# Squares of the RMS norms added on VectorE, and norm factors applied at eviction instead of ahead of the product

## The reference, cut to what matters

```python
def rms_norm(x, g):                       # _rmsnorm is the same
    return x * rsqrt(mean(x * x, -1) + 1e-6) * g

# first block
x = x + 0.5 * gt1 * swiglu(modulate(rms_norm(x, g_ffn1), sh1, sc1), w_gu1, w_down1)   # FFN 1
x = x + gt2 * hybrid_mixer(modulate(rms_norm(x, g_mix), sh2, sc2), ...)
x = x + 0.5 * gt3 * swiglu(modulate(rms_norm(x, g_ffn2), sh3, sc3), w_gu2, w_down2)   # FFN 2
x = rms_norm(x, g_final)
# second block
h = _rmsnorm(x, even_norm);  proj = h @ even_w_in       # 16 column tiles of 128
x = x + even_mixer_rest(proj) @ even_w_out              # pooling, S5 scan, gated product
h = _rmsnorm(x, odd_norm);   proj = h @ odd_w_in        # 24 tiles: value, gate, z
c = conv31(val * sigmoid(gate)) + conv_b                # 31 taps along the sequence
x = x + (silu(layer_norm(c)) * silu(z)) @ odd_w_out
return _rmsnorm(x, final_norm)
```

## Time and profile before

| | |
|---|---|
| median of three runs | 1783.36 us |
| the profiled execution: its time / its span | 1791.0 us / 1789.1 us |
| PE busy | 1632.2 us (91%), 6851 matmuls |
| DVE busy | 865.9 us (48%) |
| ACT busy | 636.8 us (36%) |
| POOL busy | 365.6 us (20%) |
| mean granted clock of PE | 0.95 |

### The profile page before, as it was taken

The page is one execution under the profiler, slowest core; times in us unless marked ns, Lnnn a source line. Parts: engine busy times, 40 slices in busy tenths (PEclk is TensorE's granted clock), DMA queues, the critical chain, the costliest instruction groups (busy, mean ns, idle before and its releaser), DMA issues. The chain is left out here.

```text
span 1789.1 us, 18560 instructions
## 1 busy us (share of the span) xinstructions
PE 1632.2 (91%) x6851; PEld 1203.2 (67%) x6851; DVE 865.9 (48%) x1190; ACT 636.8 (36%) x907; POOL 365.6 (20%) x469
## 2 busy tenths in 40 slices
PE   4899999998999998889999999999899999988377
PEld 2688888886775554235688888888477776766155
DVE  4777246333533335454433433432444344699844
ACT  3322112223335542443433212222442223666442
POOL 3011000000000000002000878510001100799700
PEclk9899999999999997789999999999899999999689
DMA  9677435322321111002233243463032122222101
GB/s 350 192 268 264 144 108 170 94 93 69 93 67 34 36 42 47 1 0 54 61 116 95 97 132 102 128 220 94 24 107 95 49 85 59 84 82 81 37 24 47
DMA packets 202194, 176.33 MB, mean 99 GB/s; under 512 B 6907, under 2 KB 181319, under 8 KB 201606
## 3 DMA queue, kind: packets, MB, share of 16 engines
q1 hardware_dynamic: 186902, 121.87, 22.9%
q0 software_dynamic: 14064, 51.34, 8.2%
q10 hardware_dynamic: 1152, 2.10, 0.3%
HBM read 166.90 MB, written 8.39 MB: 98 GB/s over the span
## 5 line engine op out<-in xcount | busy, mean ns | idle before, releaser
L1706 PE MATMUL ps<-h_hi,w_hi 128*128 128x512 f32 x1224 | 491.8, 402 | 39.4 <-DVE h_lo L1142 27.2
L1707 PE MATMUL ps<-h_lo,w_hi 128*128 128x512 f32 x1224 | 482.6, 394 | 0.0
L1708 PE MATMUL ps<-h_hi,w_lo 128*128 128x512 f32 x1224 | 482.1, 394 | 0.0
L1102 DVE TENSOR_TENSOR w_lo<-w_stage,w_hi 128x1024 fp32r<-128x1024 f32 x225 | 297.5, 1335 | 316.0 <-ACT w_hi L729 313.7
L1706 PEld LDWEIGHTS ps<-h_hi,w_hi 128*128 128x128 f32 x1224 | 233.4, 191 | 112.6 <-issue 64.1
L729 ACT ACTIVATE w_hi<-w_stage 128x1024 fp32r<-128x1024 f32 x225 | 231.0, 1048 | 200.3 <-PE ps L1708 188.3
L1708 PEld LDWEIGHTS ps<-h_hi,w_lo 128*128 128x128 f32 x1224 | 233.2, 191 | 50.2
L1707 PEld LDWEIGHTS ps<-h_lo,w_hi 128*128 128x128 f32 x1224 | 233.6, 191 | 46.6 <-issue 0.2
L1706 PE MATMUL ps<-a_hi,w_hi 128*128 128x512 f32 x544 | 225.4, 414 | 19.2 <-DVE a_lo L1644 12.8
L1707 PE MATMUL ps<-a_lo,w_hi 128*128 128x512 f32 x544 | 214.4, 394 | 0.0
L1708 PE MATMUL ps<-a_hi,w_lo 128*128 128x512 f32 x544 | 214.3, 394 | 0.0
(11 more groups left out here) (365 smaller groups left out, 1612.1 us busy)
## 6 DMA issues: line engine op xcount, KB each, us to landing
w_stage<-in_w_gu SPq DMA_DIRECT2D x88, 512.0 KB, 4.4
ada_w<-in_w_ada POOLq DMA_DIRECT2D x72, 512.0 KB, 6.4
w_stage<-in_w_down SPq DMA_DIRECT2D x44, 512.0 KB, 3.7
w_stage<-in_w_in SPq DMA_DIRECT2D x24, 512.0 KB, 3.8
w_stage<-in_odd_w_in SPq DMA_DIRECT2D x24, 512.0 KB, 3.7
w_stage<-in_even_w_in SPq DMA_DIRECT2D x16, 512.0 KB, 3.9
w_stage<-in_w_out SPq DMA_DIRECT2D x8, 512.0 KB, 4.0
mats<-mats_d POOLq DMA_DIRECT2D x4, 1024.0 KB, 7.8
```

What stands on the lines that cost most here:

```text
L1102: dve.tensor_tensor(w_lo[:, c % RING], w_in[:, c % RING], w_hi[:, c % RING].bitcast(F32), ALU.subtract).then_inc(w_split, 1)
L1706: pe.matmul(bank, w_hi[:, slot, k], rhs_hi, start=start, stop=False, skip_group_check=True)
L1707: pe.matmul(bank, w_hi[:, slot, k], rhs_lo, start=False, stop=False, skip_group_check=True)
L1708: return pe.matmul(bank, w_lo[:, slot, k], rhs_hi, start=False, stop=stop, skip_group_check=True)
```

## The change

- `square` now writes the first square into `rs` and the later ones into `sq`; DVE adds them there (`add_square`) for norms 1, 2, final, odd and last, and PE does two matmuls with ones per norm (`norm_total`) instead of eight. The table of functions is loaded ahead of the first square.
- End of FFN 2: ACT writes `h_hi` from the unnormalised `xT` times `gg` (final gain times even gain) and two squares per tile, for the final and for the even norm; DVE adds both kinds and writes `h_lo` (`scaled_lo`). The even mixer starts with these rows. Both factors come from one chain of Ln and Exp (`final_and_even_rs`), DVE writes the normalised `xT` and the common factor, and DVE takes all 16 tiles from PSUM with a multiplication by it (`take`). ACT's Silu then works in place.
- Odd mixer: its first two tiles (gate, value) are made from unnormalised rows in the same way and multiplied by the factor when taken; normalised rows are written into the upper half of `cv` and into `h_hi`, `h_lo` for the other 22 tiles.
- Last norm: ACT multiplies `xT` by the gain, PE transposes the tiles within the output product (`turn_out`), the sums are taken by rows (eight small matmuls with one column), and the factor per row is applied as the banks are copied out. The four stores take 256 columns of all 512 rows each instead of 128 full rows.

The diff, cut to its core (indentation reduced):

```diff
@@ -478,10 +497,11 @@
     load(0, T_ODD + n, cols_of(a["odd_w_in_2"][0], [D, 0, 2 * D][n % 3] + n // 3 * P))
 for n in range(KT):
     load(0, T_OOUT + n, rows_of(a["odd_w_out_2"][0], n))
-for st in range(ST):
-    sp.wait_ge(out_copied[0], st + 1)
-    sp.wait_ge(out_copied[1], st + 1)
-    sp.dma_start(out[st * P:(st + 1) * P, :], o_rows[:, st]).then_inc(out_stored, 16)
+for c in range(ST):
+    sp.wait_ge(out_copied[0], c + 1 if c < ST - 1 else ST + 1)
+    sp.wait_ge(out_copied[1], min(c + 1, ST - 1))
+    at = slice(c * 2 * P, (c + 1) * 2 * P)
+    sp.dma_start(out.rearrange("(t p) d -> p t d", p=P)[:, :, at], o_rows[:, :, at]).then_inc(out_stored, 16)
 sp.wait_ge(out_stored, 16 * ST)
...
+def two_squares(kt):
+    if kt == 0:
+        act.preload_act_table_set("natural_log_exp_and_others")
+    if kt >= 2:
+        act.wait_ge(sq_added, added(N_EVEN, kt - 1))
+    act.activation(rs[:] if kt == 0 else sq[:, 0], xT[:, kt], ACT.Square).then_inc(sq_ready, 1)
+    act.activation(tmp[:, 0] if kt == 0 else sq[:, 1], xT[:, kt], ACT.Square,
+                   scale=cols[:, G_FINAL + kt:G_FINAL + kt + 1]).then_inc(sq_ready, 1)
...
+def scaled_hi(kt, g):
+    act.activation(h_hi[:, kt], xT[:, kt], ACT.Copy, scale=g[:, kt:kt + 1]).then_inc(h_hi_ready, 1)
...
-    act.wait_ge(sq_used, (n + 1) * KT)
-    act.activation(rs[:], ps[0][:], ACT.Ln, bias=eps[:], scale=1.0 / D).then_inc(ln_ready, 1)
...
+        act.preload_act_table_set("natural_log_exp_and_others")
+        act.wait_ge(sq_used, KT)
+    else:
+        act.wait_ge(sq_used, SUMMED[n])
+    act.activation(rs[:], ps[3 if n == N_ODD else 0][:], ACT.Ln, bias=eps[:], scale=1.0 / D).then_inc(ln_ready, 1)
...
+def final_and_even_rs():
+    act.wait_ge(sq_used, SUMMED[N_FIN])
+    act.activation(tmp2[:, 0], ps[0][:], ACT.Ln, bias=eps[:], scale=1.0 / D).then_inc(ln_ready, 1)
+    act.wait_ge(ln_ready, N_FIN + 1)
+    act.activation(tmp2[:, 1], tmp2[:, 0], ACT.Exp, scale=-1.0).then_inc(fin_chain, 1)
+    act.wait_ge(fin_chain, 1)
+    act.activation(tmp2[:, 0], tmp2[:, 0], ACT.Exp, scale=-0.5).then_inc(rs_ready, 1)
+    act.wait_ge(fin_chain, 2)
+    act.activation(tmp2[:, 1], tmp2[:, 1], ACT.Ln, bias=eps[:], scale=1.0 / D).then_inc(ln_ready, 1)
+    act.wait_ge(ln_ready, N_EVEN + 1)
+    act.activation(tmp2[:, 1], tmp2[:, 1], ACT.Exp, scale=-0.5).then_inc(rs_ready, 1)
...
@@ -781,7 +838,13 @@
                     act.wait_ge(wb_stored[par], 16 * 4)
             for kt in range(KT):
                 act.wait_ge(x_new, X_FFN[n] + KT + kt + 1)
-                square(norm_after, kt)
+                if norm_after == N_FIN:
+                    if kt == 0:
+                        act.wait_ge(gs_ready, 4)
+                    scaled_hi(kt, gg)
+                    two_squares(kt)
+                else:
+                    square(norm_after, kt)
         hi(0, t1 + 12)
...
-            act.activation(us[:, n], bank, ACT.Copy).then_inc(even_read, 1)
         elif n < 12 and n % 2 == 0:
-            act.activation(zp[(n - 4) // 2], bank, ACT.Silu).then_inc(even_read, 1)
-        elif n < 12:
-            g = (n - 5) // 2
-            act.wait_ge(pads_zero, 1)
-            upto(act, pool_mixed, g - 1)
-            act.activation(pv[:, g % 2, 16:], bank, ACT.Copy).then_inc(even_read, 1)
-        else:
-            act.activation(zs[:, n - 12], bank, ACT.Silu).then_inc(even_read, 1)
+            act.wait_ge(even_read, n + 1)
+            act.activation(zp[(n - 4) // 2], zp[(n - 4) // 2], ACT.Silu).then_inc(z_ready, 1)
+        elif n >= 12:
+            act.wait_ge(even_read, n + 1)
+            act.activation(zs[:, n - 12], zs[:, n - 12], ACT.Silu).then_inc(z_ready, 1)
         t = n - 2
         if 0 <= t < 4:
...
-    for n in range(3 * KT):
+    for n in range(2):
         hi(0, T_ODD + n + 2)
+    norm_rs(N_ODD)
+    for kt in range(KT):
+        act.wait_ge(hn_ready, 3 * KT + kt + 1)
+        if kt < KT - 1:
+            act.wait_ge(pair_read, kt + 1)
+        else:
+            act.wait_ge(w_used, T_ODD + 2)
+        act.activation(h_hi[:, kt], cv[:, 4 + kt % 4], ACT.Copy).then_inc(h_hi_ready, 1)
+    act.wait_ge(odd_read, 1)
+    act.activation(tmp[:, 0], tmp[:, 0], ACT.Tanh, scale=0.5).then_inc(odd_read, 1)
...
@@ -1062,24 +1131,25 @@
 norm_rs(2)
 modulate(2, sublayer(2)[1])
 ffn(1, N_FIN, set_up)
-norm_rs(N_FIN)
...
+final_and_even_rs()
 even_mixer()
 project_out(T_EOUT, X_EVEN, N_ODD)
-norm_rs(N_ODD)
-modulate(4, None)
 odd_mixer()
 for kt in range(KT):
     act.wait_ge(x_new, X_ODD + kt + 1)
     square(N_LAST, kt)
-norm_rs(N_LAST)
-for st in range(ST):
-    act.wait_ge(out_t, KT)
-    act.activation(o_rows[:, st, 0:S], ps[2 * st][:], ACT.Copy).then_inc(out_copied[0], 1)
+    act.activation(xT[:, kt], xT[:, kt], ACT.Copy, scale=cols[:, G_LAST + kt:G_LAST + kt + 1]).then_inc(fin_ready, 1)
+act.wait_ge(sq_used, SUMMED[N_LAST])
+act.activation(rcol[:], ps[7][:, 0:ST], ACT.Ln, bias=eps[:], scale=1.0 / D).then_inc(ln_ready, 1)
+act.wait_ge(ln_ready, N_LAST + 1)
+act.activation(rcol[:], rcol[:], ACT.Exp, scale=-0.5).then_inc(rs_ready, 1)
+act.wait_ge(rs_ready, N_LAST + 1)
+for kt in (1, 3, 5):
+    act.wait_ge(out_t, kt + 1)
+    for st in range(ST):
+        ins = act.activation(o_rows[:, st, kt * P:(kt + 1) * P], ps[kt][:, st * P:(st + 1) * P], ACT.Copy,
+                             scale=rcol[:, st:st + 1])
+    ins.then_inc(out_copied[1], 1)
...
+def add_square(n, kt):
+    if 1 <= kt < KT - 1:
+        dve.wait_ge(sq_ready, squares(n, kt))
+        acc, src = (tmp[:, 0], sq[:, 1]) if n == N_EVEN else (rs[:], sq[:, 0 if n == N_FIN else kt % 2])
+        if kt > 1:
+            dve.wait_ge(sq_added, added(n, kt - 1))
+        else:
+            dve.wait_ge(sq_ready, squares(n, 0))
+        dve.tensor_tensor(acc, acc, src, ALU.add).then_inc(sq_added, 1)
+def scaled_lo(m, kt, g):
+    dve.wait_ge(h_hi_ready, m * KT + kt + 1)
+    dve.scalar_tensor_tensor(h_lo[:, kt], xT[:, kt], g[:, kt:kt + 1], h_hi[:, kt].bitcast(F32),
+                             ALU.mult, ALU.subtract).then_inc(h_ready, 1)
...
                                      xT[:, kt], ALU.mult, ALU.add).then_inc(x_new, 1)
+            if half and n == 0:
+                add_square(1, kt - 1)
+            if half and n == 1 and kt:
+                add_square(N_FIN, kt - 1)
+                add_square(N_EVEN, kt - 1)
+                scaled_lo(3, kt - 1, gg)
+        if half and n == 1:
+            scaled_lo(3, KT - 1, gg)
         lo(0, t1 + 12)
...
+    def take(n):
+        dve.wait_ge(w_used, T_EVEN + n + 1)
+        if n < 4:
...
+        dve.tensor_tensor(dst, ps[{0: 2, 1: 6}.get(n, n % 2)][:], rs[:], ALU.mult).then_inc(even_read, 1)
+    dve.wait_ge(rs_ready, N_FIN + 1)
+    dve.wait_ge(fin_chain, 1)
+    dve.tensor_tensor(tmp2[:, 1], tmp2[:, 1], ps[1][:], ALU.mult).then_inc(fin_chain, 1)
+    for kt in range(KT):
+        dve.scalar_tensor_tensor(xT[:, kt], xT[:, kt], cols[:, G_FINAL + kt:G_FINAL + kt + 1], tmp2[:, 0],
+                                 ALU.mult, ALU.mult).then_inc(x_new, 1)
+        if kt == 3:
+            lo(0, T_EVEN + 2)
+    dve.wait_ge(rs_ready, N_EVEN + 1)
+    link(dve.tensor_tensor(rs[:], tmp2[:, 1], tmp2[:, 0], ALU.mult))
     for n in range(GP + 2):
+        if 1 <= n < EVEN_IN:
+            lo(0, T_EVEN + n + 2)
         if n < EVEN_IN:
-            lo(0, T_EVEN + n + 2)
+            take(n)
         if n in (4, 6, 8, 10):
-            if n == 4:
-                dve.wait_ge(h_ready, 4 * KT)
             states((n - 4) // 2)
...
+    for kt in range(KT + 2):
+        if kt < KT:
+            if kt >= 4:
+                dve.wait_ge(h_ready, 5 * KT + kt - 3)
+            dve.scalar_tensor_tensor(cv[:, 4 + kt % 4], xT[:, kt], cols[:, G_ODD + kt:G_ODD + kt + 1], rs[:],
+                                     ALU.mult, ALU.mult).then_inc(hn_ready, 1)
+        if kt >= 2:
+            j = kt - 2
+            dve.wait_ge(h_hi_ready, 5 * KT + j + 1)
+            dve.tensor_tensor(h_lo[:, j], cv[:, 4 + j % 4], h_hi[:, j].bitcast(F32),
+                              ALU.subtract).then_inc(h_ready, 1)
+        if kt == 3:
+            lo(0, T_ODD + 3)
+    dve.wait_ge(w_used, T_ODD + 2)
+    dve.tensor_tensor(tmp[:, 0], ps[0][:], rs[:], ALU.mult).then_inc(odd_read, 1)
+    dve.tensor_tensor(gb[:, 0, TAPS - 1:], ps[1][:], rs[:], ALU.mult).then_inc(pair_read, 1)
     dve.wait_ge(cw_t, 1)
     dve.wait_ge(mix_ready, 2 * KT)
...
-    dve.scalar_tensor_tensor(xT[:, kt], xT[:, kt], cols[:, G_LAST + kt:G_LAST + kt + 1], rs[:],
-                             ALU.mult, ALU.mult).then_inc(fin_ready, 1)
-for st in range(ST):
-    dve.wait_ge(out_t, KT)
-    dve.tensor_copy(o_rows[:, st, S:], ps[2 * st + 1][:]).then_inc(out_copied[1], 1)
+for kt in (0, 2, 4, 6, 7):
+    dve.wait_ge(out_t, kt + 1)
+    dve.tensor_tensor(o_rows[:, :, kt * P:(kt + 1) * P], ps[kt % 7][:].rearrange("p (t q) -> p t q", q=P),
+                      rcol[:].unsqueeze(2).to_broadcast([P, ST, P]), ALU.mult).then_inc(out_copied[0], 1)
```

(68 more changed lines are left out.)

122 lines of the change are left out of this document (72 added, 50 removed).

## The result

The changed kernel takes 1755.11 us in the median of 4 runs (1751.45 to 1757.01), the kernel before 1784.36 us (1778.57 to 1788.19). The ratio is 0.9834, 95% interval [0.9814, 0.9854], so 29.6 us faster (26 to 33). Five later runs of the same kernel gave 1755.44 us and 0.9812 [0.9788, 0.9836]. Forecast were 1744 us and a gain of 39.5. The direction and the places were right; the measured gain is a quarter smaller than the forecast one. Between the two profiled spans lie 35.8 us, more than between the medians. 3.8 of them are start-up: FFN 1's first product stands at 52.13 us in the profile of before and at 48.34 here, but over the fourteen traces of this study it moves between 47.9 and 52.5 us in old and new kernels alike. Start-up apart, 32.0 us lie between the two.

The account below looks back on a forecast made before the run. PE was taken as the bound, busy 1632.2 of 1789.1 us, with POOL's start deciding in the odd mixer. Gains 6.0 + 5.1 + 13.0 + 8.7 + 6.7 = 39.5 us took the median from 1783.4 to 1744, range 1731 to 1762.

Parts of the forecast that it names:

- Parts 1 and 2: Norm sums at FFN 1's end and the mixer's output product: shorter PE stream, gains of 6.0 and 5.1 us.
- part 4: Even mixer's output product to POOL's first add: 5.5 us from the stream plus 3.2 behind it, 8.7 us.
- Part 3: End of FFN 2 to even mixer's third tile: 16.2 us saved, less two losses (2.4 and 0.8), gain 13.0 us.
- Part 5: Last stage: transposes replace sums in the stream, 1.5 us, and the end comes 5.2 us earlier; gain 6.7 us.
- I carry the difference over unchanged: Whole kernel: the profiled execution, 0.4% above the median, was used for the sum, its difference from the median kept.
- All of those named for a right forecast: Third even tile 37 to 40 us after first addition; two-matmul sums; POOL's add at 23 to 26; last stage 12 to 14.
- none of those for a wrong one: PE idle for DVE evictions; tile periods near 2.95 and 6.35; POOL's adds over 160 us; 1 KB rows below 300 GB/s.
- A: Even mixer: DVE becomes the bound, four scans cost 2.2 us each, 9 us, time 1753; chance 0.11.
- B: Drains: weights or additions pace them, the sums were filling; four times 5.5 us returned, time 1766; chance 0.07.
- C: PE's clock holds through the new gaps and DVE keeps up: 8 us better, 1736; chance 0.13.
- D: Odd mixer: more POOL adds become long beside DVE operations, 0.87 us each, up to 72 us and 1816; chance 0.02.

Follow-up runs that it names:

- part 3 alone: Kernel before with only the code from FFN 2's end to the even mixer's third tile changed: 1775.0 us, ratio 0.9943.
- experiment 6: Changed kernel with Parts 1 and 2 undone, eight sums of norms 1 and 2 back in PE's stream: 1758.95 us.
- experiment 8: Changed kernel with 20 idle matmuls in the gaps of the even transition: 1750.9 us, ratio 0.9810.
- experiments 10 and 11: Changed kernel with evictions, taps' weights, tanh and join moved into the odd mixer's normalised rows; the second also issues taps ahead of ScalarE's waits: 1755.5 and 1750.3 us.
- part 5's runs: Kernel before with only the last norm moved to the transposed output: 1779.9 us, ratio 0.9980.
- the early join: Changed kernel with the odd mixer's pair evictions, taps' weights, tanh and join moved into the middle of the normalised rows: 1755.5 us, ratio 0.9810.

## Why the prediction was right in its steps and too large in its sum

**Parts 1 and 2, norm sums: mechanism right, count wrong.** The step "Of the eight sums of a norm six lie between product tiles, which is 5.5 us, and two in the tail" failed. In the earlier trace rows one sum is x2 and the row at the last block is x6: three sums. Five lie between tiles, three in the tail from which I then counted again. One sum of 0.91 us is thus priced twice. Forecast 6.0, 5.1 and the 5.5 of part 4; less 0.91 each: 5.1, 4.2, 4.6. Measured: 4.8, 3.8 and 4.5 (even output product, 53.6 us on average of four traces with the sums in it and 49.1 of ten without).

**Part 3: right, 12 for 13.0.** Chain and times fit (last squares 20.6 us behind the first addition for 20.3, end of the sums 24.4 for 25.6, third tile 36.9 for 38.3). PE ran the sums at full clock in this execution; in others of the same code the third tile came at 38.6. Behind it 4.0 us were lost for the 3.2 that I had taken off. From first addition to output product: 205.5 us (two traces) and 202.0 (two) without part 3, by the clock, 191.8 in the changed kernel. That is 12 us below the mean of the four; part 3 alone, with 193.4, gives 12.0 against before.

**Part 4: right, 7.7 for 8.7.** Behind the product 3.2 us were to be gained, and 27.4 became 24.2; the stream term was short by the double count. The Silu load was exposed at its duration: 1500.02 plus 1.28, and the next operation at 1501.31. That agrees with the trace's reading in the prediction and not with the rule of the Trainium skill ("ScalarE: Activation LUTs", What ACT_TABLE_LOAD costs): no drain of 1.38 us stands here, behind the load or ahead of it.

**Part 5: right, partly by luck.** 7.0 us (2.1 in the stream, 4.9 behind it) for 6.7. The six sums in the stream were again five, but the transposes took 0.47 us a tile there (a tile with them 2.52 us, its nine matmuls 2.04), not the 0.66 taken from the earlier trace rows: 5 x 0.44 = 2.2 for the 6 x 0.25 = 1.5 of the forecast. The two errors went opposite ways.

**The sum** of the five by the traces is 8.6 + 12 + 7.7 + 7.0 = 35.3, at one clock 36.9; the forecast's 39.5 less 2.7 for the double count is 36.8. **What then failed** is the step that compared it with the medians: "I carry the difference over unchanged". It takes the 390 us between the norms, whose code stays, as constant in time. They aren't. By experiment 6, parts 1 and 2 are worth 3.8 us in the medians for 9.2 at one clock, with 0.0035 less of clock. The traces place 3.3 us of that between the norms on average (7.5 in the profiled execution); where the other 2 us are lost isn't shown. I had looked for half clock only at the gap that I was making (part 3).

**The signs.** All of those named for a right forecast came (third tile 36.9 us behind the first addition, 0.1 us under the 37 to 40; POOL 24.2; last stage 13.4), and none of those for a wrong one.

**The rivals.** A (evictions) refuted by experiment 8 and by PE's waits, of which none is for an eviction. B refuted: the drain's tiles stand at PE's own pace, five sums went at full price. C (clock holds): its PE half came true for the totals in this execution, but the clock as a whole went the other way. D refuted: 21 long adds and 152.2 us as before; in experiments 10 and 11, where VectorE's work was moved beside POOL's, the adds did get longer, as the Trainium skill ("SBUF — State Buffer", 🔬 SBUF: two separate sides) has it, by 0.5 us in all in the first and 2.3 in the second.

**What stays open.** Which feature of parts 1 and 2 makes the clock lower in stages whose code is unchanged: the gaps of 1.6 and 4.3 us, or the mere shift in time. That it was 68.3 us of half clock in both traces with idle matmuls, but also in two of seven without, doesn't decide. Open too is the low clock of part 5's runs, which are without parts 1 and 2: a low clock isn't theirs alone, though the changed kernel without them, part 5 included, had 0.9532.

## What to carry to other kernels

Count a removed instruction in one place only: read the count at the end of a row before you say how many lie in the stream and how many in the tail. When PE's gaps get fewer or shorter, price the clock of the stages that you did not touch as well; compare runs at an equal mean clock to estimate what the instructions are worth (a shorter span lowers the mean by itself), and medians to see what the user gets. And where an engine is the bound, an earlier start pays only when its feeder's queue holds no wait for a third engine ahead of its operands.

## What was not expected of the hardware

- The run's time goes with its mean granted clock, with 1.1 us of scatter over some 140 runs; 1.50 us for each 0.001. How much of that is the clock's doing and how much a longer wait that lowers the mean isn't separated.
- Idle matmuls of 128 columns in gaps of 1.6 and 4.3 us, where PE would have waited anyway, took away 6.8 us of half clock behind each norm (granted clock 1.00 for 0.58), and the norms' stages stayed at 68.1 and 51.7 us.
- In attention PE is busy for 114.4 of 130.0 us in before, and yet its granted clock is 0.79:

```profile
698.35:828.33 129.98, 114.41 (x275) 42.76 (x275) 68.69 (x168) 53.71 (x105) 0.00 (x0) 0.79 0.00 1
```

- VectorE's split of weights took 2.30 us for 1.22 beside POOL's adds in the early join (at most 2.15 beside them in before), and POOL's longest add, beside the splits of the rows, 2.67 for 1.29.
